# Feed-forward's first stage as ten groups of four tiles, with a seven-product scheme applied twice

## What is computed

```python
xn = rmsnorm(h, norm_ffn_w[l])
gate_up = xn @ w_ffn_in[l]                      # 1024 -> 2 x 2816
g_ff, u_ff = jnp.split(gate_up, [D_FF], axis=-1)
h = h + ((jax.nn.silu(g_ff) * u_ff) @ w_ffn_out[l]).astype(h.dtype)
return rmsnorm(h, norm_f_w)
```

## Time and profile before

| | |
|---|---|
| three executions | 4385.97, 4393.68, 4398.97 us, median 4393.68 |
| profiled execution, its span | 4395.4 us from the first to the last instruction |
| TensorE busy | 4283.2 us |
| VectorE, ScalarE busy | 2299.6 us, 1028.6 us |
| mean granted TensorE clock | 0.991 of full speed |

### The profile page before, as it was taken

How to read it: one execution, slowest core, us unless ns; L and a number is a source line. 1 busy time by engine, 2 the same in 40 slices (tenths; PEclk the granted TensorE clock), 3 DMA queues, 4 the chain that set the end, 5 groups by cost and what they waited for, 6 DMA issues and landing times.

```text
span 4395.4 us, 39060 instructions
## 1 busy us (share of the span) xinstructions
PE 4283.2 (97%) x15948; PEld 2143.6 (49%) x15948; DVE 2299.6 (52%) x2768; ACT 1028.6 (23%) x1378; POOL 52.7 (1%) x43
## 2 busy tenths in 40 slices
PE   7999999999999999999999999999999999999998
PEld 3446666643444444454555554544444444444444
DVE  4455555533555588854566757557433543333312
ACT  3135555412222100002334323333100110000000
POOL 0000000001110000000000000000000000000000
PEclk9999999999999999999999999999999999999999
DMA  6210000220333422222111111131311311111211
GB/s 262 86 35 6 11 11 6 68 107 30 100 111 101 168 91 91 82 92 77 39 49 44 39 58 53 48 139 70 121 43 34 110 58 39 48 40 47 89 38 55
DMA packets 114174, 307.15 MB, mean 70 GB/s; under 512 B 26021, under 2 KB 44197, under 8 KB 109258
## 3 DMA queue, kind: packets, MB, share of 16 engines
q1 hardware_dynamic: 97068, 293.11, 18.8%
q10 hardware_dynamic: 16928, 11.54, 0.8%
HBM read 241.11 MB, written 63.50 MB: 69 GB/s over the span
## 4 chain that ended last, share of the span: by engine, by line
PE 64%; DVE 9%; issue 1%; ACT 1%; POOL 0%; DMA 0%; DVEq 0%; SPq 0%; POOLq 0%
PE late_dense L132 15%; PE late_dense L2472 14%; PE late_four L4108 11%; PE late_two L4108 6%; PE late_four L4338 3%; PE late_four L1661 3%; PE late_four L2998 2%; PE late_dense L4338 2%; PE late_two L4338 1%; PE late_four L1907 1%; PE late_four L1642 1%; PE late_two L1855 1%; DVE arena L2237 0%; DVE arena L2229 0%; DVE arena L2247 0%
## 5 line engine op out<-in xcount | busy, mean ns | idle before, releaser
L132 PE MATMUL late_dense<-arena 128*128 128x512 f32 x2216 | 964.9, 594 | 3.1 <-DVE arena L3929 1.9
L132 PEld LDWEIGHTS late_dense<-arena 128*128 128x128 f32 x2216 | 420.6, 191 | 527.9 <-issue 522.0
L2472 PE MATMUL late_dense<-arena 128*128 128x512 f32 x1512 | 672.3, 598 | 3.2 <-DVE arena L2545 1.7
L4108 PE MATMUL late_four<-arena 128*128 128x512 f32 x1160 | 504.5, 592 | 0.0
L2472 PEld LDWEIGHTS late_dense<-arena 128*128 128x128 f32 x1512 | 281.1, 191 | 330.4 <-issue 326.7
L4108 PEld LDWEIGHTS late_four<-arena 128*128 128x128 f32 x1160 | 220.4, 190 | 277.4 <-issue 273.8
L4157 DVE TENSOR_TENSOR arena<-late_four,arena 128x512 f32<-128x512 f32 x145 | 98.8, 690 | 299.1 <-PE late_four L4108 295.0
L4108 PE MATMUL late_two<-arena 128*128 128x512 f32 x576 | 253.4, 592 | 0.0
L864 PE MATMUL attn_dense<-matrices,arena 128*128 128x128 f32 x1280 | 187.4, 282 | 19.1 <-ACT arena L910 16.6
L4108 PEld LDWEIGHTS late_two<-arena 128*128 128x128 f32 x576 | 109.4, 190 | 137.8 <-issue 136.3
L132 PE MATMUL attn_dense<-arena 128*128 128x512 f32 x384 | 172.3, 603 | 3.6 <-ACT arena L662 2.1
(11 more groups left out here) (431 smaller groups left out, 5199.8 us busy)
## 6 DMA issues: line engine op xcount, KB each, us to landing
arena<-in_ada_w SPq DMA_DIRECT2D x12, 2048.0 KB, 7.6
arena<-in_w_ffn_in SPq DMA_DIRECT2D x44, 512.0 KB, 4.1
arena<-in_hy_w_in SPq DMA_DIRECT2D x32, 512.0 KB, 3.3
spectrum<-arena SPq DMA_DIRECT2D x8, 2048.0 KB, 8.1
arena<-spectrum SPq DMA_DIRECT2D x8, 2048.0 KB, 11.3
arena<-in_w_gates SPq DMA_DIRECT2D x32, 512.0 KB, 3.7
spill<-arena SPq DMA_DIRECT2D x26, 512.0 KB, 4.9
arena<-spill SPq DMA_DIRECT2D x26, 512.0 KB, 4.4
```

The lines of the kernel that those rows point to most:

```text
L132: mm = pe.matmul(self.ps[:, n % SEG], self.wbuf[:, slot, k], job.rhs[:, k, cols], start=(job.first and k == 0), stop=(job.last and k == kt ...
L2472: mm = pe.matmul(I.bank(M, name, i), left[:, k], right, start=(first and k == 0), stop=(k == 3), skip_group_check=True)
L4108: mm = pe.matmul(product_bank(M, name, i), left[:, k], right[:, k], start=(k == 0), stop=(k == 3))
```

## The change

The twenty pairs become ten quads (`QUADS`): tiles g and u of two consecutive n, 512 output columns in all. The scheme of seven products is applied twice. On the outer level the left matrix of a quad (four tiles by eight slices) and `xn` are cut in 2x2 blocks; seven blocks (`LEFTS` by `RIGHTS`) per quad, 70 in all (`BLOCKS`). Each block is again cut in 2x2: seven products p1 to p7 of two matmuls with 256 moving columns (`block_product_pe`). VectorE makes four small sums (128x256) of each block's weights (`parts`), and for each of the seven right blocks four small turns, once. Within a block p1, p6, p7 and p4 accumulate in the same half of a PSUM bank; in between ScalarE copies the state reached (`hold`), and at the end `corner`; VectorE adds (`join`). The results of the blocks are added on the outer level (`level_sum`, 128x1024), then Silu and `gate`. TensorE interleaves two blocks (`deep_pe`).

Since the extra operands take the room, 17 of the 22 result tiles are stored to DRAM (`F.spill`) and come back during the last quad (`back` in `output_sp`). In the output stage P2 takes its slices in another order, and the turns T1 to T4 are made in another order, T2 in two pieces and T3 as T2 - b11. The two plain pairs, all before them and the rest of the output stage stay.

The diff, cut to its core (`load_x` and `load` there are loads of x and of output weights; `quarters` and `left_quarters` cut a block in 2x2; `row_free` makes ScalarE and VectorE wait until the row that a block's result goes into has been read; `silu` does the Silus of four of the seven blocks; `plain` is the old multiplication of the plain pairs):

```diff
...
-PAIRS = MIXED + FT - PLAIN
+QUADS = (FT - PLAIN) // 2
+BLOCKS = 7 * QUADS
...
+STEP_ORDER = ("p1", "p7", "p2", "p3", "p6", "p4", "p5")
+OF_NEXT = ("p1", "p2", "p6", "p5")
+LEFTS = ("A11", "A12", "S4", "S2", "S1", "S3", "A22")
+RIGHTS = ("B11", "B21", "B22", "T2", "T1", "T3", "T4")
+LEVEL_ROWS = (0, 1, 2, 3, 4, 5, 5)
+LEVEL_SUMS = ("C11", "U2", "V", "C12", "C22", "U3", "C21")
...
+SPILLED_HIDDEN = 17
+QUARTER = BANK // 2
...
+        self.S1, self.S2, self.S4 = [sums(39), sums(40)], sums(41), sums(42)
...
+        self.small_sums = [[ring[:, s, n] for n in range(3)] for s in range(4)]
+        self.kept = [rows[:, 46 + n] for n in range(3)]
+        self.level = [rows[:, r] for r in (12, 13, 14, 15, 16, 53)]
+        four, two, dense = mem.four, mem.two, mem.dense
+        self.banks = [(four[:, 0], four[:, 1]), (four[:, 2], four[:, 3]), (two[:, low], two[:, high]), (dense[:, 0], dense[:, 1])]
+        self.loaded, self.loaded_before = [M.raw_in, M.lg_in], 64
...
+def deep_sp(sp, F):
+    M = F.M
+
+    def load(q):
+        for n in range(2):
+            sp.dma_start(F.sets[q % 2][:, 2 * n:2 * n + 2].rearrange("p t k c -> p (t k) c"),
+                         F.weights[PLAIN + 2 * q + n]).then_inc(F.loaded[q % 2], 16)
+
+    def store(n):
+        if n < SPILLED_HIDDEN:
+            sp.dma_start(F.spill[n], F.out_row(n)).then_inc(F.stored, 16)
+
+    sp.wait_ge(M.ffn_norm.totaled, M.ffn_norm.parts + 2)
+    load(0)
     for n in range(PLAIN):
+        for half in range(SEG):
+            sp.wait_ge(M.dense.emptied[half], M.dense.evicted_at(f"u{n}"))
+        store(n)
+    for q in range(QUADS):
+        if q:
+            sp.wait_ge(F.made, F.made_at(q - 1, "C21"))
+            store(PLAIN + 2 * q - 1)
+        if q >= 1 and q + 1 < QUADS:
+            sp.wait_ge(F.product, F.product_at(7 * q - 1, "p4"))
+        if q + 1 < QUADS:
+            load(q + 1)
+        sp.wait_ge(F.made, F.made_at(q, "C12"))
+        store(PLAIN + 2 * q)
...
+    left, right = {"p1": (a11, b11), "p2": (a12, b21), "p6": (s2, t2), "p5": (s1, b12), "p7": (a21, t3), "p3": (s4, b22),
+                   "p4": (a22, t4)}[name]
+    chain, beside = F.banks[b % 4]
...
+        pe.wait_ge(F.parts_made, F.parts_made_before + 4 * b + 4)
+        if b < 7:
+            pe.wait_ge(F.turned, F.turned_at(f"{RIGHTS[b]} 3"))
+        if b >= 4:
+            pe.wait_ge(F.cornered, F.cornered_before + b - 3)
+    elif name == "p2":
+        if b >= 4:
+            pe.wait_ge(F.joined, F.joined_before + b - 3)
+    elif name == "p6":
+        pe.wait_ge(F.held1, F.held1_before + b + 1)
+    elif name == "p5":
+        if b < 3:
+            pe.wait_ge(F.moved, F.moved_before + b + 1)
+    elif name == "p7":
+        pe.wait_ge(F.held6, F.held6_before + b + 1)
+    elif name == "p3":
+        pe.wait_ge(F.held5, F.held5_before + b + 1)
+    else:
+        pe.wait_ge(F.held7, F.held7_before + b + 1)
+    out = beside[:, 0:QUARTER] if name == "p2" else beside[:, QUARTER:BANK] if name in ("p5", "p3") else chain[:, 0:QUARTER]
+    for k in range(2):
+        mm = pe.matmul(out, left[:, k], right[:, k], start=(name in ("p1", "p2", "p5") and k == 0), stop=(k == 1),
+                       skip_group_check=True)
+    mm.then_inc(F.product, 1)
+
...
+def deep_pe(pe, F):
+    for half in range(SEG):
+        pe.wait_ge(F.M.dense.emptied[half], F.M.dense.evicted_at(f"u{PLAIN - 1}"))
+    for b in range(BLOCKS + 1):
+        for name in STEP_ORDER:
+            if name in OF_NEXT:
+                if b < BLOCKS:
+                    block_product_pe(pe, F, b, name)
+            elif b:
+                block_product_pe(pe, F, b - 1, name)
...
+    def hold(b, name):
+        chain, beside = F.banks[b % 4]
+        kept = F.kept[b % 3]
+        act.wait_ge(F.product, F.product_at(b, name))
+        if name == "p1":
+            if b >= 3:
+                act.wait_ge(F.centred, F.centred_before + b - 2)
+            elif b:
+                act.wait_ge(F.moved, F.moved_before + b + 1)
+            act.activation(kept[:, 0:QUARTER], chain[:, 0:QUARTER], ACT.Copy).then_inc(F.held1, 1)
+        elif name == "p6":
+            act.activation(kept[:, QUARTER:BANK], chain[:, 0:QUARTER], ACT.Copy).then_inc(F.held6, 1)
+        elif name == "p5":
...
+    def corner(b):
+        act.wait_ge(F.product, F.product_at(b, "p4"))
+        row_free(act, F, b)
+        act.activation(F.row_of(b)[:, BANK:BANK + QUARTER], F.banks[b % 4][0][:, 0:QUARTER], ACT.Copy).then_inc(F.cornered, 1)
...
+    for b in range(BLOCKS + 2):
...
+        if b < BLOCKS:
+            hold(b, "p1")
+        if 1 <= b <= BLOCKS:
+            hold(b - 1, "p7")
+        if b < BLOCKS:
+            hold(b, "p6")
+        if 1 <= b <= BLOCKS:
+            corner(b - 1)
+        if b >= 2:
+            silu(b - 2)
+        if b < BLOCKS:
+            hold(b, "p5")
+
...
+        dve.tensor_tensor(t3, x22, x12, ALU.subtract).then_inc(F.turned, 1)
+        dve.tensor_tensor(t1, x12, x11, ALU.subtract).then_inc(F.turned, 1)
+        dve.wait_ge(F.turned, F.turned_at(f"{name} 1"))
+        dve.tensor_tensor(t2, x22, t1, ALU.subtract).then_inc(F.turned, 1)
+        dve.wait_ge(F.turned, F.turned_at(f"{name} 2"))
+        dve.tensor_tensor(t4, x21, t2, ALU.subtract).then_inc(F.turned, 1)
+
...
+        if name == "S1":
+            dve.wait_ge(F.loaded[q % 2], F.loaded_before + 32 * (q // 2 + 1))
+            dve.tensor_tensor(F.S1[q % 2], a21, a22, ALU.add).then_inc(F.sums_made, 1)
+        elif name == "S3":
+            dve.tensor_tensor(a21, a11, a21, ALU.subtract).then_inc(F.sums_made, 1)
+        elif name == "S2":
+            dve.wait_ge(F.sums_made, F.sums_made_before + 4 * q + 1)
+            if q:
+                dve.wait_ge(F.product, F.product_at(7 * q - 4, "p4"))
+            dve.tensor_tensor(F.S2, F.S1[q % 2], a11, ALU.subtract).then_inc(F.sums_made, 1)
+        else:
+            dve.wait_ge(F.sums_made, F.sums_made_before + 4 * q + 3)
+            if q:
+                dve.wait_ge(F.product, F.product_at(7 * q - 5, "p4"))
+            dve.tensor_tensor(F.S4, a12, F.S2, ALU.subtract).then_inc(F.sums_made, 1)
+
...
+        if b >= 4:
+            dve.wait_ge(F.product, F.product_at(b - 4, "p4"))
+        dve.wait_ge(F.sums_made, F.sums_made_before + 4 * q + 4)
+        dve.tensor_tensor(s1, x21, x22, ALU.add).then_inc(F.parts_made, 1)
+        dve.tensor_tensor(x21, x11, x21, ALU.subtract).then_inc(F.parts_made, 1)
+        dve.wait_ge(F.parts_made, F.parts_made_before + 4 * b + 1)
+        dve.tensor_tensor(s2, s1, x11, ALU.subtract).then_inc(F.parts_made, 1)
+        dve.wait_ge(F.parts_made, F.parts_made_before + 4 * b + 3)
+        dve.tensor_tensor(s4, x12, s2, ALU.subtract).then_inc(F.parts_made, 1)
+
+    def join(b):
+        row, kept = F.row_of(b), F.kept[b % 3]
+        row_free(dve, F, b)
+        dve.wait_ge(F.product, F.product_at(b, "p3"))
+        dve.wait_ge(F.held6, F.held6_before + b + 1)
+        dve.tensor_tensor(row[:, 0:BANK], F.banks[b % 4][1], kept[:, 0:BANK], ALU.add).then_inc(F.joined, 1)
+        dve.wait_ge(F.held7, F.held7_before + b + 1)
+        dve.tensor_tensor(row[:, BANK + QUARTER:L], kept[:, BANK:BANK + QUARTER], kept[:, BANK + QUARTER:L],
+                          ALU.add).then_inc(F.centred, 1)
...
+        out, one, two = {"C11": (1, 1, 0), "U2": (3, 3, 0), "V": (4, 4, 3), "C12": (2, 2, 4), "C22": (4, 4, 5), "U3": (3, 3, 5),
+                         "C21": (5, 5, 3)}[name]
...
+        dve.tensor_tensor(F.level[out], F.level[one], F.level[two], ALU.add).then_inc(F.summed, 1)
...
+        if stored > 0 and n >= 5:
+            dve.wait_ge(F.stored, F.stored_before + 16 * min(n - 4, SPILLED_HIDDEN))
...
+    turn_whole("T3", right["T3"], right["B22"], b12)
+    turn_whole("T1", F.first_turn, b12, right["B11"])
+    dve.wait_ge(F.turned, F.turned_at("T1"))
+    turn_whole("T2", right["T2"], right["B22"], F.first_turn)
+    dve.wait_ge(F.turned, F.turned_at("T2"))
+    turn_whole("T4", right["T4"], right["B21"], right["T2"])
+    turn_small("B11")
+    plain(0)
+    for name in ("S1", "S3", "S2", "S4"):
+        sums(0, name)
+    parts(0)
+    turn_small("B21")
+    turn_small("B22")
+    parts(1)
+    parts(2)
+    turn_small("T2")
+    plain(1)
+    turn_small("T3")
+    dve.wait_ge(F.turned, F.turned_at("T4"))
+    turn_small("T4")
+    for b in range(BLOCKS):
+        q, j = divmod(b, 7)
+        join(b)
+        dve.wait_ge(F.cornered, F.cornered_before + b + 1)
+        dve.wait_ge(F.centred, F.centred_before + b + 1)
+        for name in {1: ("C11",), 3: ("U2",), 4: ("V", "C12"), 5: ("C22", "U3"), 6: ("C21",)}.get(j, ()):
+            level_sum(q, name)
+        if b == 0:
+            dve.wait_ge(dense.filled, SEG * len(dense.jobs))
+            dve.tensor_copy(right["T1"], F.first_turn).then_inc(F.turned, 1)
+        elif b == 1:
+            dve.wait_ge(F.turned, F.turned_at("T1 back"))
+            turn_small("T1")
+        if j in (2, 5, 6):
```

(89 more changed lines are left out.)

239 lines of the change are left out of this document (166 added, 73 removed).

## The result

| | executions, us | median | ratio to before |
|---|---|---|---|
| before | 4385.97, 4392.25, 4393.68, 4398.97 | 4392.97 | |
| changed | 4360.66, 4361.66, 4362.09, 4366.12 | 4361.88 | 0.9931 (0.9918 to 0.9944) |

The account below looks back on a forecast made before the run. The prediction took TensorE's matmul records to bound the stage: -56.8 us of records, +0.9 at the start seam and -0.3 at the end make -56.2, so 4337.5 us from the median 4393.7, range 4328 to 4360.

Parts of the forecast that it names:

- TensorE's term: In the replaced stage, 1960 records of 0.2163 us take 423.9 us in place of 480.7: 56.8 us less.
- The boundary: Between the new stage's 490 four-record groups: taken as 0, with 0 to 0.09 us each kept for the range.
- rivals 1 and 5: Group boundaries: 1, waits cost 10 to 44 us, chance 0.10; 5, weight loads lie open, 97 us, chance 0.04.
- ScalarE and VectorE: In the new stage both keep ahead of TensorE: 16 and 32.7 of 42.4 us per quad, VectorE's tightest slack 1.0 us.
- Rival 2: VectorE becomes the bound in blocks 3 to 5 of each quad: 12 to 25 us, 4350 to 4363, chance 0.07.
- The clock in the stage: Granted clock stays 1.00 in the new stage; the rival, a falling clock, costs 25 us, 4362, chance 0.03.
- The seams without the returning tiles: At the new stage's start +0.9 us; at its end 0.8 us idle but the 1.16 us P6 wait goes, net -0.3.
- The returning tiles: Before the output, 8.5 MB of tiles load from 21.6 us before the stage's end, hidden under it at 400 GB/s.
- rival 3: Tiles come back late at the last seam, before the output: 6 to 12 us, 4344 to 4350, chance 0.04.

Follow-up runs that it names:

- e3: e1 plus four added 512-column sums in VectorE's queue in block 4 of each of nine quads: 4351.7 us, 0.9905 of before.
- e1: Changed kernel without SyncE's empty wait for gate C12 in the last two quads, where no tile is stored: 4339.7 us, 0.9878 of before.
- e2: Changed kernel with SyncE's last loop wait on the last quad's gate C11 in place of C12: 4344.1 us, 0.9887 of before.
- e5: Changed kernel with SyncE's last loop wait on block 67's last product in place of gate C12: 4353.0 us, 0.9906 of before.
- e6: Changed kernel with SyncE's last loop wait on block 65's last product in place of gate C12: 4343.6 us, 0.9887 of before.
- e4: e1 with TensorE's waits at the new stage's start and end moved later or to earlier blocks' results: 4333.7 us, 0.9865 of before.

## Why the prediction was wrong

- **TensorE's term, right.** 1960 records at 0.2159 us, 422.9 us from the first to the last start and 423.1 with the last record's own 0.22, for 423.9 forecast. Against 480.7 that is -57.6 instead of -56.8.
- **The boundary, right.** In the changed kernel 1958 of the 1959 distances are 215 or 216 ns and one, the first, 291. A boundary after four records of 256 columns costs nothing; rivals 1 and 5 fall.
- **ScalarE and VectorE, right.** Small sums start 0.34 us apart, 0.45 where one needs the other (3653.55, 3653.90, 3654.23, 3654.68 us in the changed kernel), 0.33 and 0.45 forecast; the copies take 0.38 us; the slack is 1.05 us for 1.0 (e3). Rival 2 falls, but it was near. Only the VectorE time that I said the profile would show (360 us) was too high: 323, near the 327 of the prediction's own sum of 32.7 a quad.
- **The clock in the stage, right.** It is granted at 1.00 through 423 us with four pairs of banks cycled. The Trainium skill (TensorE: Matmul & The Clock Gate, "A second HAM failure mode: psum-queue depth-cycling") tells of a clock that swings under such cycling with brief idle times between groups; by this trace it does not happen here, where there are no idle times between the groups.
- **The seams without the returning tiles, right.** 0.90 us at the start for 0.9; at the end 0.67 us in e1 for 0.8 (the profile names ScalarE's copy, which ended at 4043.54; VectorE's join ended at 4043.69, 0.10 us before P1, so it was the join, as forecast); no wait at P6 any more; T1 starts 3.7 us after the last product in e1 (3.8 forecast; the product counted to its last record's start plus 0.22).
- **The returning tiles, wrong, and this is the step that failed:** "The 17 tiles that come back (8.5 MB), four x tiles and the last weights are issued in five steps from 21.6 us before the end. [...] Hidden". They were issued from 2.6 us after the end (the last weights at 4042.20, the first tile at 4042.72, the stage's last product ended at 4039.60), behind five pieces of weights of which the first went out 0.1 us after it. I read the waits beside these loads and not the one ahead of them in the same queue, which `deep_sp` leaves behind for a tile that is not stored. The price was 27.4 us of the rest: 24.2 idle, 2.3 of clock at the output's start, and 0.9 of clock in the last normalisation. The last goes along with a late hand-off in e2 too, but not in e5, so it isn't shown to belong to it. The price that I gave for this cover, "at half the rate the first eight would come 6 us late", and rival 3 with its 6 to 12 us asked about the rate; the rate was as read, 410 GB/s, and what was late was the start. A late start has no such bound: it costs the whole 24.5 us from opening to landing.

With that wait gone (e1) the sum holds: 716.6 us of rest for 718.1, 4339.7 us for 4337.5.

## What to carry to other kernels

When loads are to hide under a stage, list every wait ahead of them in their queue, also those whose guarded work is empty in the last turns of a loop; a wait with nothing behind it is still a wait, and a trace names the transfer, not the wait, as what was late. Look at the issue time before the rate: issues that run back to back just after an engine's last instruction are a queue that was shut. And an engine at 57% may have 1 us of slack at one place per turn; it is the due times there, not the share, that tell.

## What the runs showed of the hardware that was not expected

Here an idle TensorE cost more than its idle time. After 3.64, 5.43, 15.07 and 24.85 us without a matmul the next four to seven records of 512 columns ran at the lower level of the clock (0.85 us for 0.43), 2.0 to 3.1 us lost; after 0.67 us none did, nor after 1.16 us in the kernel before. The loss did not grow from 5.43 to 24.85 us, and was largest (3.1 us, seven records) after the shortest of these idle times, 3.64 us; why is open.

Nor does the length of the idle time alone decide. The 2.42 us before the last normalisation's eight short records are the same in every kernel, to 0.01. In the changed kernel and e2 all eight then ran at the lower level (0.21 us apart), in the kernel before and e6 some of them, in e1, e3, e4 and e5 none (0.11 us apart). What differs is not shown. Nor is it separated whether the full DMA queue has a part in the four long waits at P1: it moved 410 GB/s over the slow records, 367 to 400 over the same stretch of e1, e3 and e4, where the clock held.
